# Loading each expert's down weights in two transfers of 4096 byte rows in place of one of 8192 byte rows

## The reference

```
def moe_ffn(h, w_router, router_bias, w_gate, w_up, w_down, ws_gate, ws_up, ws_down):
    ...
    for e0 in range(0, N_EXPERTS, EXPERT_BLOCK):
        sl = slice(e0, e0 + EXPERT_BLOCK)
        hg = jnp.einsum('nd,edf->nef', t, w_gate[sl])
        hu = jnp.einsum('nd,edf->nef', t, w_up[sl])
        hw = jax.nn.silu(hg) * hu * combine[:, sl, None]
        routed = routed + jnp.einsum('nef,efd->nd', hw, w_down[sl])
    shared = (jax.nn.silu(t @ ws_gate) * (t @ ws_up)) @ ws_down
    return (routed + shared).reshape(B, S, D)
```

## Time and profile before

| | before |
|---|---|
| median of 3 runs | 1117.52 us (1117.26 to 1118.98) |
| the profiled execution: its own time | 1113.93 us |
| the profiled execution: span from first to last instruction | 1112.0 us |
| TensorE busy, share of the span | 971.8 us, 87% |
| VectorE busy | 905.2 us, 81% |
| ScalarE busy | 602.3 us, 54% |
| GpSimd busy | 278.4 us, 25% |
| SyncE's DMA queue (q1): packets, MB | 64240, 248.03 |
| GpSimd's DMA queue (q0): packets, MB | 19056, 36.89 |
| transfers of `w_d`: number, size, median to landing | 64, 1024.0 KB, 8.6 us |
| transfers of `w_gu`: number, size | 256, 512.0 KB |

### The profile page before, as it was taken

The page is one execution under the profiler, slowest core; times in us unless marked ns, Lnnn a source line. Parts: engine busy times, 40 slices in busy tenths (PEclk is TensorE's granted clock), DMA queues, the critical chain, the costliest instruction groups (busy, mean ns, idle before and its releaser), DMA issues.

```text
span 1112.0 us, 14197 instructions
## 1 busy us (share of the span) xinstructions
PE 971.8 (87%) x4335; PEld 745.7 (67%) x4336; DVE 905.2 (81%) x1280; ACT 602.3 (54%) x948; POOL 278.4 (25%) x186
## 2 busy tenths in 40 slices
PE   3797899898999979898999988989897999898895
PEld 1354375586788657677777777777676777677684
DVE  3687877754566878998999999999998899898894
ACT  1123153466113046676777766667675767676672
POOL 1004105130000202323234232332323232324232
PEclk9899899889999989999999999999999999999897
DMA  9976402200027278999999999999999999999973
GB/s 310 393 280 232 151 1 76 104 2 1 19 89 276 67 294 268 374 318 339 325 340 359 344 333 339 326 337 333 327 349 327 309 333 356 351 327 350 341 257 59
DMA packets 86232, 286.79 MB, mean 258 GB/s; under 512 B 18052, under 2 KB 18564, under 8 KB 77112
## 3 DMA queue, kind: packets, MB, share of 16 engines
q1 hardware_dynamic: 64240, 248.03, 61.1%
q0 software_dynamic: 19056, 36.89, 13.2%
q10 hardware_dynamic: 2904, 1.48, 0.5%
HBM read 283.04 MB, written 37.88 MB: 289 GB/s over the span
## 4 chain that ended last, share of the span: by engine, by line
DMA 49%; PE 29%; DVE 11%; issue 6%; ACT 1%; SPq 1%; POOL 1%; POOLq 0%; DVEq 0%; ACTq 0%
DMA out<-oute,src_tab 44%; PE bank L633 5%; PE bank L574 4%; PE bank L575 4%; PE bank L576 4%; DMA xe<-h_rows,src_tab 3%; DMA ada_w<-in_w_ada 2%; DVE ada_acc L1234 2%; PE bank L787 2%; PE bank L708 2%; PE bank L725 1%; DVE gu_low L1466 1%; DVE q_sb L1313 1%; PE bank L804 1%; PE bank L716 1%
## 5 line engine op out<-in xcount | busy, mean ns | idle before, releaser
L1466 DVE TENSOR_TENSOR gu_low<-w_gu,gu_high 128x1024 fp32r<-128x1024 f32 x256 | 301.4, 1218 | 10.6 <-ACT gu_high L1103 5.4
L1103 ACT CAST gu_high<-w_gu 128x1024 fp32r<-128x1024 f32 x256 | 256.6, 1055 | 62.8 <-PE bank L576 57.2
L530 POOL DMA_INDIRECT out<-oute,src_tab x64 | 128.9, 2015 | 465.0 <-DMA out<-oute,src_tab 357.5
L574 PE MATMUL bank<-gu_high,xeT_high 128*128 128x512 f32 x512 | 208.1, 406 | 2.8 <-DVE xeT_low L1466 2.6
L576 PE MATMUL bank<-gu_high,xeT_low 128*128 128x512 f32 x512 | 202.1, 395 | 0.0
L575 PE MATMUL bank<-gu_low,xeT_high 128*128 128x512 f32 x512 | 201.8, 394 | 0.0
L1466 DVE TENSOR_TENSOR d_low<-w_d,d_high 128x1024 fp32r<-128x1024 f32 x128 | 150.4, 1216 | 0.0
L1109 ACT CAST d_high<-w_d 128x1024 fp32r<-128x1024 f32 x128 | 128.1, 1053 | 18.0 <-PE bank L576 18.0
L820 PE MATMUL bank<-ident,xe 128*128 128x128 f32 x512 | 73.5, 288 | 60.3 <-DMA xe<-h_rows,src_tab 58.4
L820 PEld LDWEIGHTS bank<-ident,xe 128*128 128x128 f32 x512 | 64.5, 194 | 81.3 <-issue 77.6
L574 PE MATMUL bank<-d_high,hwT_high 128*128 128x512 f32 x256 | 112.3, 439 | 6.7 <-DVE hwT_low L1466 6.5
(11 more groups left out here) (278 smaller groups left out, 1291.6 us busy)
## 6 DMA issues: line engine op xcount, KB each, us to landing
w_gu<-in_w_exp_gate SPq DMA_DIRECT2D x128, 512.0 KB
w_gu<-in_w_exp_up SPq DMA_DIRECT2D x128, 512.0 KB
w_d<-in_w_exp_down SPq DMA_DIRECT2D x64, 1024.0 KB, 8.6
ada_w<-in_w_ada SPq DMA_DIRECT2D x12, 2048.0 KB, 11.9
w_out_sb<-in_w_out SPq DMA_DIRECT2D x2, 2048.0 KB, 7.2
w_lat_sb<-in_w_in SPq DMA_DIRECT2D x1, 2688.0 KB, 21.9
x_sb<-in_x SPq DMA_DIRECT2D x1, 2048.0 KB, 24.2
w_v_sb<-in_w_in SPq DMA_DIRECT2D x1, 2048.0 KB, 10.3
```

The lines of the kernel that those rows point to most:

```text
L530: pool.indirect_dma_start(out_rows, bass.IndirectOffsetOnAxis(ap=rows, axis=0), oute[i][:], None, bounds_check=last_row, oob_is_err=False, ...
L574: pe.matmul(dst, xh, wh, start=start, stop=False)
L1103: act.copy(gu_high[half][:, m], w_gu[half][i][:, m]).then_inc(gu_high_ok[half], 1)
L1466: return dve.tensor_tensor(low, whole, high.bitcast(F32), ALU.subtract)
```

## The change

`load_down` issues `FC` = 2 transfers, one for each of the two rows of a partition, in place of one. Each moves 512 KB in runs of 4096 bytes, at a stride of 8192 bytes in memory, and both add 16 to the same semaphore. ScalarE's waits on `ld_d` count 32 for a load in place of 16. Nothing else is altered.

```
             def load_down(e, i):
-                sp.dma_start(w_d[i][:], a["w_exp_down"][0, bass.ds(e, 1)].rearrange("o (p c) n -> p (o c) n", c=FC)).then_inc(ld_d[i], 16)
+                src = a["w_exp_down"][0, bass.ds(e, 1)].rearrange("o (p c) n -> p (o c) n", c=FC)
+                for j in range(FC):
+                    sp.dma_start(w_d[i][:, j], src[:, j]).then_inc(ld_d[i], 16)
...
             def down_high_of(E):
-                down_high(E[1] % 2, times(pairs(E), 16), num(E))
+                down_high(E[1] % 2, times(pairs(E), 16 * FC), num(E))
...
-                down_high(0, i * 16 + 16 * (EXTRA0 + 1), n)
+                down_high(0, i * (16 * FC) + 16 * FC * (EXTRA0 + 1), n)
```

## The result

| | before | change |
|---|---|---|
| median, same chip | 1118.25 us (1117.26 to 1119.68, 4 runs) | 1100.11 us (1091.76 to 1109.08, 4 runs) |
| the profiled execution: time, span | 1113.93, 1112.0 us | 1091.82, 1090.0 us |
| time of the change over time of before | | 0.976, 95% interval 0.974 to 0.979 |

Two of the four runs of the change (1108.4 and 1109.1) ran at a lower clock than the other two and are left out of the ratio, which is why it is lower than that of the medians.

The account below looks back on a forecast made before the run. The loop of scatter, landing and next scatter was taken as the bound, VectorE close behind. 50 x (0.22 - 0.11) = 5.5 us off 1117.5 gave 1112 us, range 1096 to 1127; a small gain had chance 0.30.

Parts of the forecast that it names:

- What bounds the kernel: Expert stage: each scatter waits for the one before to land; a shorter landing gives up to some 0.6 us per period.
- Issues on SyncE, two transfers: SyncE's loop: one more DMA issue per expert, some 0.4 us with its address instruction, fits in idle time; cost 0.
- Row cost, 0.11 us for each expert: DMA engines: two 4 KB rows cost 0.014 us more than one 8 KB row; 0.11 us if the scatter follows all of w_d.
- Turns: DMA engines alternating row by row between scatter and w_d: a scattered row waits 0.149 us less, at most 0.22 us per period.
- 50 periods: Expert stage: scatters, of 64, that wait for the previous landing; the net gain per period was multiplied by this count.
- Slack of w_d, "cost 0": w_d lands 9.9 us before ScalarE reads it, so issuing its second half 0.4 us later costs 0.
- Nothing moves: Rival, chance 0.25: engines serve all of w_d first whatever its rows; gain and cost vanish or cancel, 1117.5 us.
- slower by the row cost: Rival, chance 0.17: scatter always waits for the whole of w_d; 0.11 us per expert stays, 7 us slower, 1124.5 us.
- A second start-up: Rival, chance 0.13: the second w_d transfer brings its own gap, scatter lands 0.34 us later, 22 us slower, 1139 us.
- A large gain by bursts: Rival, chance 0.15: w_d passes as bursts; two shorter ones let the scatter in sooner, 30 to 37 us gained, 1084 us.
- The moment of the load: Caveat, no size: the scatter's place may depend on when w_d is issued, its second half now 0.4 us later, not row size.

Follow-up runs that it names:

- the repeat: The changed kernel, unaltered, timed again on another chip beside the kernel before: ratio 0.985 (0.979 to 0.990).
- the last kernel: The changed kernel with w_gu loaded in eight transfers of 256 KB with 2048-byte rows instead of four of 512 KB: 0.978 of the kernel before.

## Why the prediction was right and wrong

**What bounds the kernel: right.** The loop of scatter, landing, next scatter had 44% of the span and has 29% now; without scatters the period falls to the 9.92 us that VectorE needs.

**Issues on SyncE, two transfers: right.** No run shows a cost of the second issue, and the number of transfers moved nothing between two and four.

**Row cost, 0.11 us for each expert: not on the path.** It was taken off the gain in full, for the case that the scatter stands behind all of w_d. The packets' own times (medians, 500 to 1000 us) are 309 ns for 8192 bytes, 159 for 4096 and 84 for 2048, so the price was near: 128 x (2 x 159 - 309) / 16 = 0.07 us for each expert, and 0.22 us with rows of 2048. But the first scattered row comes no later in the change (4.65, now 4.60), and 2048-byte rows, with three times the cost, gained more.

**Turns: the right mechanism, by the evidence, and the term that was mis-sized.** This is the step that failed: "24 of the 8 KB rows are left (267 - 243): at most 24 x 0.149 / 16 = 0.22 us sooner", less 0.11, in 50 periods. What the runs showed is a period shorter by 0.32 us, 63 times, and a landing sooner by 0.4 us.

The 24 was not even right for the period it was read from. The stretch from 709 to 712 was taken as one in which both are served. Cut at 711 us it falls apart: first the part to 711, then 711 to 715.

```profile
DMA packets 159, 0.68 MB, mean 340 GB/s; under 512 B 17, under 2 KB 17, under 8 KB 135
...
q1 hardware_dynamic: 159, 0.68, 101.2%
```

```profile
DMA packets 433, 1.13 MB, mean 283 GB/s; under 512 B 161, under 2 KB 161, under 8 KB 433
...
q0 software_dynamic: 257, 0.49, 45.5%
```

All 24 large rows (159 - 135) were served before 711 us, with no packet of the scatter's queue among them. From 711 us on, when the scatter's rows pass, all 433 packets are under 8 KB. So this period had no large row beside the scatter, and by the prediction's own reckoning nothing to gain. It wasn't the usual one. Counted by packets over all 64 scatters, 40 large rows on average are served between the first and the last scattered row (median 34.5, from 0 to 128), and 40 x 0.149 / 16 = 0.37 us. The measured stretch from first to last became 0.35 us shorter in the change and 0.36 in the kernel with small rows alone, with its start unmoved in both; in the repeat it became 0.57 us shorter and began 0.20 later. So the size fits, and it would have made a forecast of 50 x 0.37 = 19 us before the cost of the rows.

The premise under it was wrong too: "in the usual period, w_d is issued before the scatter" holds for 25 of 61 periods; in the median w_d follows by 0.35 us. Most of its rows are served ahead of the scatter's all the same, because those come some 5 us after the start. And 50 periods was too simple a count: in the change only 44 scatters still wait for a landing, since VectorE's oute has taken over in six more.

**Slack of w_d, "cost 0": right for w_d, wrong for the loads together.** It had been read as a reserve of 9.9 us that nothing would use. A scatter that is served sooner takes from the loads what it gains, and a quicker period asks for weights sooner: in the profiled execution of the change w_gu is waited for 28.3 us where it was not at all. On the other chip the change had no such wait, so this is a border it stands at. With 2048-byte rows the waits are there each time (67.7 and 52.0 us for w_gu), and the gain stops before VectorE's floor.

**The rivals.** *Nothing moves* and *slower by the row cost* are refuted by the ratio. *A second start-up* is refuted by the time of four transfers, which equals that of two. *A large gain by bursts*, which needs two transfers and a period 0.6 us shorter, doesn't fit either: the period fell by 0.32 us, and one transfer with small rows gains already. *The moment of the load*, my own caveat, is not what the change lives by, since one transfer issued as before gains and a load issued behind the scatter keeps the gain; but moving the load by some 5 us changes landing and slack alike, so the moment matters by itself. It isn't cleanly apart from the row size either: against the scatter's start w_d's issue moved from 0.35 us (median) to 0.8 in the change and 1.5 with 2048-byte rows, though no line that orders these issues was altered.

**What stays open.** That the row size, without a second transfer, brings the scatter in sooner is shown. That the gain of 4096-byte rows comes between the scatter's first row and its last, and not ahead of the first, is what the packets show in three kernels. That it comes turn by turn, one row against one row, is argued from the size. With 2048-byte rows the first scattered row comes 0.41 us sooner as well, and neither turns nor these runs say why; the later issue of w_d is one candidate. No kernel got w_d wholly behind the scatter's rows with its slack kept. And the half per cent between the change and its single-transfer form is inside the intervals.

**The best version** here is w_d in 2048-byte rows: 0.970 of before, in two transfers or four, 1.5% better than the change beside it.

## What to carry to other kernels

Where a small transfer that something waits for shares the DMA engines with bulk loads that have slack, the bulk loads' row size is a dial between the two: smaller rows bring the small transfer in sooner, and it pays until what the loads are waited for eats up what the small one gains. Look at both sides of it, the landing of the small one and the waits for the loads. First waits for loads aren't yet the point to stop: with 67.7 us of them the 2048-byte rows of w_d were still the best version, with 131.9 us in the last kernel nothing was left over the change. And before a term is multiplied by 50 periods, read it in all of them, or in many, and cut the stretch small enough to see that the two things in it really stand side by side: my 24 rows had passed before the scatter's first.

## What the hardware did that I had not expected

Two transfers of 64 partitions in place of one of 128, same rows and bytes, slowed every load: 234 GB/s in place of 336, 68 us of an engine for each MB in place of 44, and the kernel by 22%.

A semaphore increment that GpSimd's program has behind the scatter and the gather after it releases another queue as soon as 0.5 us after the scatter's start (705.46, load issued 705.99), although the profile shows GpSimd busy with such a scatter for 1.9 us (median) and with the gather only from 707.79. In this kernel it didn't hold the load back until the rows were out.

A row of the accumulating scatter, 4096 bytes, took 327 ns, about twice the 159 ns of a 4096-byte row of weights (medians, 500 to 1000 us of the kernel before).
